# Attention pairs: the decay tiles of ScalarE move from ahead of the next pair's exponents to behind the first taps

## What is computed

```python
# blocks of 128 queries; keys: the block, its neighbours, and 256 of context
s_loc, s_ctx = q @ k_band * scale, q @ k_ctx * scale      # masked to the band
m   = max(s_loc, s_ctx, sink)
e   = exp(s - m); den = e.sum() + exp(sink - m)
out = (e_loc @ v_band + e_ctx @ v_ctx) / den
```

```python
log_d = b[t] - b[s] + li[s]; log_d = where(tril, log_d, -inf)
dmat  = exp(log_d - m_t)                                  # one tile per step and direction
```

## Time and profile before

| | |
|---|---|
| median of three runs | 2130.36 us (2124.75 to 2131.63) |
| span of the profiled execution | 2127.8 us (the profile gives no other time for it; the median lies 2.56 us above) |
| TensorE matmul busy | 2091.4 us, 98% |
| VectorE busy | 1527.0 us, 72% |
| ScalarE busy | 905.6 us, 43% |
| GpSimd busy | 192.8 us, 9% |
| the stage with decay tiles | about 1031 to 1131 us of the span |

### The profile page before, as it was taken

How to read it: one execution, slowest core, us unless ns; L and a number is a source line. 1 busy time by engine, 2 the same in 40 slices (tenths; PEclk the granted TensorE clock), 3 DMA queues, 4 the chain that set the end, 5 groups by cost and what they waited for, 6 DMA issues and landing times.

```text
span 2127.8 us, 31643 instructions
## 1 busy us (share of the span) xinstructions
PE 2091.4 (98%) x11508; PEld 1768.0 (83%) x11510; DVE 1527.0 (72%) x2520; ACT 905.6 (43%) x1631; POOL 192.8 (9%) x212
## 2 busy tenths in 40 slices
PE   8999999999999999999999999999999999999998
PEld 4888888888888888899878878877888888888886
DVE  5778888777648878675665465866867777767787
ACT  4622222222237446542565555734532323336445
POOL 0000000000000001090111002821000000000001
PEclk9999999999999999999999999999999999999999
DMA  8144444555459664733231002732244434349773
GB/s 298 33 142 147 149 134 129 160 167 159 129 186 348 193 215 148 209 101 117 74 108 41 21 21 66 182 109 99 75 134 140 136 104 153 123 139 341 257 234 112
DMA packets 261841, 310.38 MB, mean 146 GB/s; under 512 B 19350, under 2 KB 164686, under 8 KB 261710
## 3 DMA queue, kind: packets, MB, share of 16 engines
q1 hardware_dynamic: 261422, 308.52, 45.4%
q10 hardware_dynamic: 288, 0.13, 0.0%
HBM read 242.13 MB, written 66.45 MB: 145 GB/s over the span
## 4 chain that ended last, share of the span: by engine, by line
PE 86%; DVE 4%; DMA 3%; ACT 2%; issue 1%; POOL 1%; SPq 1%; DVEq 0%; POOLq 0%; ACTq 0%
PE psum L1327 11%; PE psum L1328 11%; PE psum L1329 11%; PE psum L1527 6%; PE psum L1529 6%; PE psum L1528 6%; PE psum L2056 3%; PE psum L2058 3%; PE psum L2057 3%; PE psum L1347 2%; PE psum L1346 2%; PE psum L1345 2%; PE psum L3078 2%; PE psum L875 2%; PE psum L876 2%; PE psum L877 2%
## 5 line engine op out<-in xcount | busy, mean ns | idle before, releaser
L1327 PE MATMUL psum<-x_mix_h,x_op_h 128*128 128x512 f32 x640 | 251.2, 393 | 1.3 <-DVE v_sum L1135 1.2
L1328 PE MATMUL psum<-x_mix_l,x_op_h 128*128 128x512 f32 x640 | 249.8, 390 | 0.0
L1329 PE MATMUL psum<-x_mix_h,x_op_l 128*128 128x512 f32 x640 | 249.5, 390 | 0.0
L1527 PE MATMUL psum<-s_high 128*128 128x512 f32 x616 | 240.0, 390 | 0.3 <-DVE s_low L1514 0.3
L1528 PE MATMUL psum<-s_low,s_high 128*128 128x512 f32 x616 | 239.9, 389 | 0.0
L1529 PE MATMUL psum<-s_high,s_low 128*128 128x512 f32 x616 | 239.9, 389 | 0.0
L1514 DVE TENSOR_TENSOR s_low<-s_raw,s_high 128x1024 fp32r<-128x1024 f32 x154 | 186.9, 1217 | 50.5 <-ACT s_high L1475 50.5
L1475 ACT ACTIVATE s_high<-s_raw 128x1024 fp32r<-128x1024 f32 x154 | 161.3, 1057 | 124.1 <-PE psum L1529 56.3
L1019 ACT ACTIVATE x_op_h<-raw 128x512 fp32r<-128x512 f32 x140 | 86.1, 627 | 203.6 <-PE psum L1329 121.1
L1019 ACT ACTIVATE x_op_h<-w_sum 128x512 fp32r<-128x512 f32 x160 | 97.1, 625 | 162.9 <-DVE w_sum L997 107.1
L1327 PEld LDWEIGHTS psum<-x_mix_h,x_op_h 128*128 128x128 f32 x640 | 120.4, 188 | 25.4 <-issue 1.8
(11 more groups left out here) (408 smaller groups left out, 5069.6 us busy)
## 6 DMA issues: line engine op xcount, KB each, us to landing
raw<-in_ffn_w SPq DMA_DIRECT2D x88, 512.0 KB, 5.4
f_terms<-g_half SPq DMA_DIRECT2D x154, 256.0 KB, 2.3
s_raw<-f_terms SPq DMA_DIRECT2D x154, 256.0 KB, 3.2
s_raw<-in_ffn_w SPq DMA_DIRECT2D x154, 256.0 KB, 4.0
ada_slice<-in_w_ada SPq DMA_DIRECT2D x112, 256.0 KB, 3.1
c_raw<-in_ffn_w SPq DMA_DIRECT2D x22, 512.0 KB, 3.5
p_raw<-in_w_in SPq DMA_DIRECT2D x22, 512.0 KB, 4.0
early<-in_w_ada SPq DMA_DIRECT2D x16, 512.0 KB, 6.6
```

Of the source, the lines that this page charges most:

```text
L1327: nc.tensor.matmul(o, wh[:, k], high(k), start=i < 4 and k == 0, stop=False, skip_group_check=i > 3)
L1328: nc.tensor.matmul(o, wh[:, k], low(k), start=False, stop=False, skip_group_check=i > 3)
L1329: last = nc.tensor.matmul(o, wl[:, k], high(k), start=False, stop=k == KH - 1, skip_group_check=i > 3)
L1527: nc.tensor.matmul(o, h[:, 0, rows], h[:, 1], start=i == 0 and q in (0, 1, 6), stop=False, skip_group_check=True)
```

## The change

All decay tiles of a pair now stand where only the second stood. Of the eleven pairs with decay tiles, six had one, ahead of the exponents, and five had two, one ahead and one behind. After the change every tile stands behind the pair's exponents, result copy, sink columns and first taps. The other engines' programs are the same.

```diff
                     if at == p > 0:
                         proj_high(act, u)
-                decays = list(decays_in(p))
-                for i in decays[:1]:
-                    decay_tile_act(act, i)
                 exponent_act(act, 2 * p + 2)
                 exponent_act(act, 2 * p + 3)
                 pair_rows_act(act, p)
...
                 for j in groups_done(p):
                     group_act(act, j)
-                for i in decays[1:]:
+                for i in decays_in(p):
                     decay_tile_act(act, i)
             keep_pair_act(act, ATT_PAIRS - 1)
```

## The result

The changed kernel takes 2134.16 us (median of 20 runs, 2131.38 to 2140.2) against 2130.5 us before (20 runs, 2124.75 to 2136.96). The ratio is 1.002, with a 95% interval of 1.0013 to 1.0027: between 2.8 and 5.8 us slower. The forecast was 2133.3 us, or 2.9 us slower.

The account below looks back on a forecast made before the run. TensorE was taken to set the time, already waiting for ScalarE's copies. Late copies (+1.17, +0.81, +0.30, +0.73, +1.17, +0.25) less 1.50, with pairs 7 and 8 cancelling, gave +2.93 us: 2133.3 us, range 2127 to 2140.

Parts of the forecast that it names:

- Removed gap at pair 3: Pair 2 to 3: exponents start ahead of tile 3, so TensorE's gap for probabilities goes, -1.50 us.
- late copies at pairs 1 to 6: ScalarE's copies come late behind moved tiles: +1.17, +0.81, +0.30, +0.73 us at pairs 1 to 4, +1.17 at pair 6.
- What pair 7 gives, pair 8 takes.: Pair 7's 3.19 us gap goes, but pair 8's near copy still waits behind tile 11; its gap grows 1.02 to 4.21 us.
- the ring: Decay tiles' store and load round through GpSimd and SyncE's queue; sets tile 11's mask, forecast 2.68 us later.
- The clock: TensorE's granted clock: taken to stay at 1.00, as in the 3.19 us gap; no term in the sum.
- rival four: Clock falls in pair 8's gap, slowing matmuls by 0 to +8.4 us, half taken, +4.2: 2137.5 us; chance 0.13.
- the forecast's own signs of being wrong: Pair 8's near copy not waiting for tile 11, span below 2127, or granted clock below 1.00 between 1105 and 1115.
- Stores and loads: Stores of tiles 4 to 6 slip about 4 us each, absorbed in SyncE's 12.3 us wait ahead of the next weights.
- Rival three: Tile stores slip a round, so pairs 7 to 9 pay 4.3 us more: 2137.6 us; chance 0.10.
- One: Both gaps for probabilities go and the copies keep up, gain in full: -4.69 us, 2125.7 us; chance 0.08.
- Two: Earlier taps hide the copies of pairs 2, 4 and 6; gain and late copies cancel: 2130 us; chance 0.17.

Follow-up runs that it names:

- the further executions: Both kernels unchanged, two more profiled executions each: before 2129.81 and 2132.77 us, changed kernel 2135.53 and 2133.19 us.
- the first kernel: Kernel before with only tiles 3 and 9, of pairs 2 and 6, moved behind the taps: 2127.43 us, ratio 0.999.
- the fastest kernel: Kernel before with tiles 3 and 9 behind the taps and tiles 10 to 15 one per pair from pair 7, behind the taps: 2121.81 us.
- the costs alone: Changed kernel with tiles 3 and 9 put back ahead of the exponents: 2133.32 us, ratio 1.0017 to before.

## Why the prediction was right, and where it was not

The stretch of each pair, from its transposes to the next pair's, in us:

| pair | before | forecast | after | measured |
|---|---|---|---|---|
| 0 | 8.43 | 0 | 8.45 | +0.02 |
| 1 | 8.38 | +1.17 | 9.53 | +1.15 |
| 2 | 9.28 | +0.81 - 1.50 | 8.48 | -0.80 |
| 3 | 8.02 | +0.30 | 8.43 | +0.41 |
| 4 | 8.60 | +0.73 | 9.52 | +0.92 |
| 5 | 8.63 | 0 | 8.63 | 0 |
| 6 | 12.64 | +1.17 - 3.19 | 10.75 | -1.89 |
| 7 | 8.65 | 0 | 8.73 | +0.08 |
| 8 | 9.44 | +3.19 | 13.37 | +3.93 |
| 9 | 8.36 | +0.25 | 8.56 | +0.20 |
| 10 | 8.71 | 0 | 8.77 | +0.06 |
| sum | 99.14 | +2.93 | 103.22 | +4.08 |

- *Removed gap at pair 3, late copies at pairs 1 to 6.* Each term came out within 0.2 us. The gaps they predict (1.5, 0.8, 0.7 and 1.7 us) are in the trace as 1.49, 0.77, 0.83 and 1.67.
- *"What pair 7 gives, pair 8 takes."* Right, and shown by three kernels. With the gap at pair 7 put back the time is the same; without it, tile 10 or 11 waits for the ring at pair 8; with tile 11 out of the way of pair 8 the loss is gone. The wait behind pair 8 was mis-sized, 3.31 us for 4.21 (3.77 and 3.41 in the further executions). Some 0.5 us of the difference are the ring's: the weights' high part came 2.9 us later against the rest (forecast 2.7), but the round behind it was shorter, since a load from issue to mask took 3.44 us where before it took 3.99. The other 0.4 us are TensorE's: by the table, pair 8's transposes came so much later than forecast.
- *The clock.* This is the step that was wrong. The sum has no term for it, and rival four weighed the fall as a risk of the changed kernel alone, because the 3.19 us of the first profile had left the clock at 1.00. That was one execution. At the same gap it fell in two others of the same kernel. In the changed kernel one of the forecast's own signs of being wrong was there: a granted clock below 1.00 between 1105 and 1115, which with the offset is 1108.6 to 1118.6 (0.50 from 1114 to 1116). So the clock cost both kernels something: 1.64 us at pair 8 of the changed one in its first profile; before, the slower matmuls of pair 7 in part only fill the wait of pair 8 (the gap of 1.02 us is missing in both later executions). Of the 4.08 us in the profiled pair of executions 1.64 are the clock's, and 2.44 stand against the forecast's 2.93. That the total came out near is therefore partly luck: the wait of pair 8 was shorter than forecast, and the clock, which the sum left out, more than made up for it. On the mean of three executions of each kernel the waits of the stage alone come to 3.1 us, and only 0.5 us of the clock is left between the two.
- *Stores and loads.* Tile 4's store went out at 1070.91, with the offset 4.4 us later than before, and the slip was gone ahead of the weights, as said. Rival three did not happen.
- *The rivals.* One fell with the first kernel: the gain alone is 0.2 to 3.8 us, not 4.69. Two needed taps 1 us earlier; the copies were as late as computed. Four happened in its cause, at 1.64 us and not 4.2 on top, and in both kernels.

What stays open: why the fastest kernel's median lies 7.2 us below before and its profiled stage only 5.1. Pair 12 gives 0.65 us more. For the rest there is an estimate: its eight runs have a granted clock of 0.9960 on the mean, the 31 of before 0.9949, and a straight line through those 31 gives 1.55 us less time for 0.001 more of clock, so some 1.7 us. Part of that may be this kernel's own, since the gap at pair 7, behind which the clock fell in two of three profiles of before, is gone.

## What to carry to other kernels

An engine that works in order gives an instruction's wait to whatever stands behind it, so ask of a moved wait which work it now holds up and how much idle time it leaves behind: here the tiles left idle time ahead of the exponents for a place ahead of copies that TensorE already waited for. A gap that the chain of waits goes around is worth nothing until the chain itself is shortened; two gaps on the same engine, one behind the other, are not added before asking what sets the second. Move only the instructions that wait, and move the late ones far enough: two tiles moved behind the taps and the last six spread to one a pair gave 0.29%, where moving all eleven cost 0.2%.

## What the runs showed of the hardware

TensorE's granted clock fell to 0.50 behind a gap of 2.0 us (behind the stage: in all three executions of after and one of before), of 2.51 us (the gain alone), of 3.19 us (the costs alone), of 3.20 and 3.21 us (before) and of 3.31, 3.41 and 3.77 us (after), and stayed at 1.00 behind one gap of 3.19 us (before, first profile) and behind that of 2.0 us in two executions of before. The same gap in the same kernel can thus go either way. A fall comes on top of the gap: 1.64 us at pair 8 of the changed kernel, and at pair 7 of the kernel before 2.75 and 1.59 us (11.40 and 10.24 us of matmuls for 8.65). Of the Trainium skill, TensorE: Matmul & The Clock Gate, Part 1, the traces agree that the clock is given back by activity: it was at 1.00 again in the stretch from 1118, TensorE having been busy since 1112.53. I had not expected a gap of 2.51 us to be enough, and one of 2.0 was.
